# Choosing 128 of 144 keys by the 16 left out, and moving small steps around the pairs of an attention block

## The chip, the cores and the metric

The kernel runs on one core of a Trainium2 chip. The metric is the device time of one execution in microseconds, as the median of several. TensorE, VectorE, ScalarE, GpSimd and SyncE each work through their own list of instructions in order and wait for one another by semaphores.

## The reference, cut to what matters

Two blocks follow one another on 512 tokens of width 1024: a gated-linear-attention mixer and a state-space mixer, then a transformer block with 16 meta tokens ahead (528 tokens), whose mixer has 8 dense causal heads and 8 heads that see only 128 chosen keys. The part that the change touches:

```python
topk = min(TOPK_MAX, seq // 4)                       # 128
logits = einsum('bqhd,bkd->bqhk', q_idx, k_idx) * idx_scale
score = einsum('bqh,bqhk->bqk', w_idx, relu(logits))
score = where(causal, score, -inf)
_, sel = lax.top_k(score, topk)
valid = sel <= qpos
s = einsum('bqhd,bqkhd->bhqk', q, k[sel]) * scale    # also for the dense heads, without sel
p = softmax(where(valid, s, -inf))
o = einsum('bhqk,bqkhd->bqhd', p, v[sel])
h = h + concat(o_mla, o_dsa) @ w_o                   # h: the residual, rms-normed x of the first block
h = h + swiglu(rmsnorm(h)); out = rmsnorm(h)
```

## The kernel before, in words

Activations lie with features on the 128 partitions and tokens along the free axis. A product is three matmuls of split parts (lines 728 to 730), and each output tile goes to one of two banks of PS by turns: `open_tile` waits until the tile before the last has been read out (`slot_free`). Weights come through a ring of slots; ScalarE makes their high part (L1515), GpSimd (L2890) or VectorE (L2162) the low part.

The attention block, in the order of TensorE: query tiles of the index (qi), kk and ckv, cq and qs, beside which the 20 index scores stand (L1207); then ks, vs (three tiles), uqr (two), uqn (four), ukn (four), ukvv (three), and the 32 pairs of heads (`PAIRS`): four tiles of 128 queries, which see 144, 272, 400 and 528 keys, and for each 4 dense (mla) and 4 sparse (dsa) pairs; the first tile has its sparse pairs first.

Index scores: TensorE makes `index_scores(n)`, when relu n - 1 is done; ScalarE's relu (L1934) of score n waits for VectorE's sums of score n - 2 (`summed_up`, `acc_used`); VectorE sums into `acc`, one row of keys per query. Score units 0 to 3 are the queries 0 to 127, 4 to 7 the second tile, 8 to 11 the third, 12 to 19 the fourth. After unit 15's round VectorE splits a weight.

Choice (`select`): a round is MAX8, which finds the 8 largest of a row, and MATCH_REPLACE, which sets them to `TAKEN`. 16 rounds for each of the four tiles find 128 keys. After the last, two instructions (L2725, L2726) turn the row into a mask that also is causal. 8 rounds stand behind units 12 to 19, 32 behind the rotations (`rotate`, L2667 to L2677) of QS, KR, KS and QR, and 24 in the pairs 3 to 26, one each.

ScalarE after the index: ks (L1912), vs (L1972), QR (`evac`, L1538, with the split of the next weight ahead of the wait), a copy of the rotary keys KR to four heads' rows of Km in two steps (`rotary_keys`, L1976), the second after the first tile of Qm (L1987, L1988), then Km (L1995).

A pair p: TensorE makes the scores of p (L1315 dense, L1317 sparse), the transposes of p - 2 (L1353), the product with values of p - 3 (L1365). VectorE copies the output of p - 4 to OA (L2765), adds the mask and finds the maximum (L2784), makes a round of choice (p = 3 to 26), two reciprocals of the sums (L2771), each after its exponential, and for p = 23 to 30 scales one tile of the residual XT (L2796). ScalarE makes two exponentials (L2002) and copies the transposed weights of p - 2 (L2022, L2024). GpSimd scales the two heads by the reciprocals (L2916). The transposes of a 528-key tile also wait for the copy to OA of the pair two before them.

Then attn_out: 8 tiles, each added to XT by VectorE (L2822), which frees the bank, then the sums of squares and the split for the next stage. The first two tiles are computed side by side.

Of the kernel before, what the change touches and what calls it, by code (L numbers as in the profile page):

```python
# [2 lines left out]

# [1 line left out]

# [7 lines left out]
ALU = mybir.AluOpType  # L13
ACT = mybir.ActivationFunctionType
# [6 lines left out]
KD = D // P  # L21
# [6 lines left out]
NPAIR = T // P  # L28
# [29 lines left out]
TOPK = 128  # L58
# [3 lines left out]
LOW = -1e30  # L62
TAKEN = -3e38
# [13 lines left out]
PV_GLA, PV_BG, PV_HG, PV_S5, PV_BGLU, PV_DS, PV_FIN, PV_ATT, PV_GQ, PV_GKV, PV_FFN, PV_FIN2, PV_N = \  # L77
# [81 lines left out]
def build(nc, a, out):  # L159
# [105 lines left out]
    tiles = plan.tiles  # L265
# [23 lines left out]
    PLAIN, plain_at = {}, 0  # L289
# [7 lines left out]
    with ExitStack() as ctx:  # L297
# [25 lines left out]
        pv = keep("pv", [P, PV_N])  # L323
# [5 lines left out]
        rs1 = keep("rs1", [P, T])  # L329
# [4 lines left out]
        st = keep("st", [P, 3, 8])  # L334
        xt_off = top[0] + 31 & -32
        XT = keep("XT", [P, KD, T])
# [115 lines left out]
        VS, o = place("VS", [P, 5, DH * DHD], o)  # L452
# [3 lines left out]
        top8, o = place("top8", [P, 8], o)  # L456
        mx, o = place("mx", [P, 6, 4], o)
# [34 lines left out]
        PS = ctx.enter_context(nc.psum_tensor("PS", [P, 4, 512], F32))  # L492
# [6 lines left out]
        tile_done = sem("tile_done")  # L499
# [61 lines left out]
        def keys(i):  # L561

            return NM + (i + 1) * P
# [16 lines left out]
        FIRST_QS = len(ROTATIONS)  # L580
# [23 lines left out]


        OUT_SPLIT, FIRST_CHOICE = len(PAIRS) - 8, 3
        XT_PAIR = len(PAIRS) - KD - 1

        z_dram = nc.dram_tensor("z_gates", (DI, T), F32, kind="Internal").ap()
        g_dram = nc.dram_tensor("glu_parts", (DI, T), F32, kind="Internal").ap()  # L610
# [88 lines left out]
        def norm_applied(eng, name):  # L699

            if name == "ck":
                eng.wait_ge(xlo_ready, sum(SPLITS["ckv"]))
            elif name in SPLITS:
                eng.wait_ge(xlo_ready, sum(SPLITS[name]))
            else:
                eng.wait_ge(normed, PLAIN[name] + NORMS[name][2])
# [755 lines left out]
        def act_program(act):  # L1462
# [45 lines left out]
            def split_weights(upto):  # L1508


                while done[0] <= min(upto, len(plan.loads) - 1):
                    n = done[0]
                    done[0] += 1
                    act.wait_ge(landed[n % NSLOT], plan.value[n])
                    act.activation(ring_hi[:, n % NSLOT, 0:plan.size[n]], ring[:, n % NSLOT, 0:plan.size[n]], ACT.Copy)\  # L1515
                        .then_inc(whi_ready, 1)
# [448 lines left out]
            for i, tile in enumerate(tiles["ks"]):  # L1965
                wide(tile, KS[:, i, :])

            for i, tile in enumerate(tiles["vs"]):
                split_weights(tile.loads[-1] + 1)
                act.wait_ge(tile_done, tile.t + 1)  # L1970
                for b in range(2 if i < 2 else 1):
                    m = act.activation(VS[:, 2 * i + b, :], PS[:, 2 * tile.slot + b, :], ACT.Copy, scale=st[:, 2, 2 * i + b:2 * i + b + 1])  # L1972
                m.then_inc(slot_free[tile.slot], 1)
            def rotary_keys(j):

                ins = act.activation(Km[MNOPE:MQK, 2 * j:2 * j + 2, :],  # L1976
                                     KR[MNOPE:MQK, :].unsqueeze(1).broadcast_to([MROPE, 2, T2]), ACT.Copy)
                if j == 1:
                    ins.then_inc(kr_copied, 1)

            for i, tile in enumerate(tiles["uqr"]):
                evac(tile, QR[:, i, :], scale=-MQK ** -0.5)
            act.wait_ge(roped, KEYS_TURNED)
            rotary_keys(0)
            for i, tile in enumerate(tiles["uqn"]):
                act.wait_ge(tile_done, tile.t + 1)
                act.activation(Qm[0:MNOPE, 2 * i, :], PS[0:64, 2 * tile.slot, 0:T], ACT.Copy, scale=-MQK ** -0.5)  # L1987
                act.activation(Qm[0:MNOPE, 2 * i + 1, :], PS[64:P, 2 * tile.slot, 0:T], ACT.Copy, scale=-MQK ** -0.5)\  # L1988
                    .then_inc(slot_free[tile.slot], 1)
                if i == 0:  # L1990
                    rotary_keys(1)
            for i, tile in enumerate(tiles["ukn"]):
                act.wait_ge(tile_done, tile.t + 1)
                for h in range(2):
# [104 lines left out]
        def dve_program(dve):  # L2099
            chain = [0]  # L2100

            def link(ins):

                chain[0] += 1
                ins.then_inc(dve_chain, 1)
                dve.wait_ge(dve_chain, chain[0])
# [584 lines left out]
            def acc_of(i):  # L2691
                return acc[:, ACC_AT[i]:ACC_AT[i + 1]]

            def causal(i):
                return rt[:, C_CB + T2 - keys(i):C_CB + T2]

            def summed_up(n):
                i, hp, c0, w = INDEX[n]
                dve.wait_ge(relu_ready, n + 1)
                here = acc_of(i)[:, c0:c0 + w]  # L2700
                for h in range(2):
                    of, weight = RL[:, n % 2, h, 0:w], WI[:, i, 2 * hp + h:2 * hp + h + 1]
                    if hp == h == 0:
                        link(ts(here, of, weight, None, ALU.mult))
                    else:
                        ins = stt(out=here, in0=of, scalar=weight, in1=here, op0=ALU.mult, op1=ALU.add)
                        if h == 0:
                            link(ins)
                ins.then_inc(acc_used, 1)
                dve.wait_ge(acc_used, n + 1)  # L2710
                if hp == 3 and c0 + w == keys(i):
                    link(tt(acc_of(i), acc_of(i), causal(i), ALU.subtract))

# [1 line left out]

            def select(rounds):
                for _ in range(rounds):
                    i, last = chosen[0] // (TOPK // 8), chosen[0] % (TOPK // 8) == TOPK // 8 - 1  # L2720
                    chosen[0] += 1
                    link(dve.max(top8[:], acc_of(i)))
                    link(dve.match_replace(out=acc_of(i), in_to_replace=top8[:], in_values=acc_of(i), imm_value=TAKEN))
                    if last:
                        link(ts(acc_of(i), acc_of(i), TAKEN, 1.0, ALU.is_equal, ALU.subtract))  # L2725
                        link(stt(out=acc_of(i), in0=acc_of(i), scalar=LOW, in1=causal(i), op0=ALU.mult, op1=ALU.add))  # L2726

# [21 lines left out]
            low("ckv", 0, ssq[:, 0:T2], CKh[:, 0:T2], CKl[:, 0:T2])  # L2749
            for n in range(12, len(INDEX)):  # L2750
                summed_up(n)
                select(1)
                if n == 15:
                    low_weights(tiles["ks"][0].loads[0])
            for n, rounds in zip(range(FIRST_QS, len(ROTATIONS)), (5, 5, 4, 4, 4, 4, 3, 2, 1, 0, 0)):
                rotate(n)
                select(rounds)

# [7 lines left out]
                    .then_inc(oa_ready, 1)  # L2766

            def inverse_sums(p):
                for n in (2 * p, 2 * p + 1):
                    dve.wait_ge(exp_ready, n + 1)  # L2770
                    dve.reciprocal(mx[:, n % 6, 2:3], mx[:, n % 6, 1:2]).then_inc(rsum_ready, 1)  # L2771

            dve.wait_ge(pb_zero, 1)
            for p, (kind, i, hp) in enumerate(PAIRS):
                if p >= 4:
                    output(p - 4)
                nk = keys(i)
                bias = causal(i) if kind == "mla" else acc_of(i)
                dve.wait_ge(score_ps, p + 1)
                if p >= 3:  # L2780
                    dve.wait_ge(pT_ps, p - 2)
                for h in range(2):
                    n = 2 * p + h
                    dve.tensor_tensor_reduce(split(PB[:, n % 6, 0:nk], i), scores(p, h), split(bias, i), 1.0, -TAKEN, ALU.add, ALU.min,  # L2784
                                             mx[:, n % 6, 0:1]).then_inc(reduced, 1)
                if p == 1:
                    tile = tiles["ukvv"][2]
                    dve.wait_ge(tile_done, tile.t + 1)
                    dve.tensor_copy(Vm[:, 4, :], PS[:, 2 * tile.slot, :]).then_inc(slot_free[tile.slot], 1)
                if 0 <= p - FIRST_CHOICE < 3 * TOPK // 16:  # L2790
                    select(1)
                inverse_sums(p)
                if 0 <= p - XT_PAIR < KD:

                    k = p - XT_PAIR
                    stt(out=XT[:, k, :], in0=XT[:, k, :], scalar=pv[:, PV_FIN + k:PV_FIN + k + 1], in1=rs1[:], op0=ALU.mult, op1=ALU.mult)\  # L2796
                        .then_inc(normed, 1)
            assert chosen[0] == NPAIR * (TOPK // 8)
            output(len(PAIRS) - 4)

            for n in (2 * len(PAIRS) - 2, 2 * len(PAIRS) - 1):
# [14 lines left out]

            for i in range(4, KD):
                low("oa", i, OA[:, i, :], OAh[:, i, :], OAl[:, i, :])
            norm_applied(dve, "fin")
            for i, tile in enumerate(tiles["attn_out"]):  # L2820
                dve.wait_ge(tile_done, tile.t + 1)
                tt(XT[:, i, :], XT[:, i, :], PS[:, 2 * tile.slot, :], ALU.add).then_inc(slot_free[tile.slot], 1)  # L2822
                sum_squares("ffn", i - 1)
                if i > 0:
                    ffn_low(i - 1)
# [237 lines left out]
```

## Time and profile before

| what | us |
|---|---|
| median of 3 runs (lowest to highest) | 1667.53 (1667.22 to 1667.67) |
| span of the profiled execution | 1664.5 |
| TensorE busy | 1625.8 (98%) |
| VectorE busy | 1003.7 (60%) |
| ScalarE busy | 713.9 (43%) |
| GpSimd busy | 474.9 (29%) |

The profiled execution has no run time of its own beside its span; the runs of the kernel lie some 3 us above it. Mean granted TensorE clock 0.996. The attention block's part that the change touches lies from 1040 to 1240 us. Shares of busy time are means over stages with different limits; what ends a wait is read in the waits and timelines. In the rows, the first number is the start in us from the span's start, the second the time in us; `x2` is a merged group of two; what stands in brackets is the idle time of that engine ahead of the row and what ended it. PE is TensorE, DVE VectorE, ACT ScalarE, POOL GpSimd.

### The profile page before, as it was taken

The numbers are of one execution on the slowest core, as the hardware profiler recorded it, in microseconds if no ns is written. First come the engines' busy times: TensorE is split into PE (matmuls) and PEld (weight loads), VectorE is DVE, ScalarE is ACT, GpSimd is POOL, SyncE is SP. The second block draws the span as 40 slices with busy tenths as digits, with TensorE's granted clock in tenths as the row PEclk, the third lists the DMA queues.
The fourth block names the chain that finished last, engine by engine and source line by source line (L and its number), as shares of the span: only waits on it lengthen the run. The fifth ranks groups of instructions, "written<-read, shape, count | busy, mean of one in ns | idle before, by whom it ended". The sixth has DMA issues, their size and how long they took to land.

```text
span 1664.5 us, 24805 instructions
## 1 busy us (share of the span) xinstructions
PE 1625.8 (98%) x10072; PEld 1296.2 (78%) x10072; DVE 1003.7 (60%) x1569; ACT 713.9 (43%) x1112; POOL 474.9 (29%) x169
## 2 busy tenths in 40 slices
PE   9999999999999998999999999999999999999998
PEld 7778688888778786778887886786778888888887
DVE  4356635786999999984672755998963212222123
ACT  4482433334555567655433333327763322222122
POOL 2221124342000000000434431234773344344332
PEclk9999999999999999999999999999999999999999
DMA  5232013235655454556643321221003333322322
GB/s 177 77 101 76 27 52 99 79 101 162 141 145 142 123 150 114 119 137 212 225 134 115 101 74 52 76 57 52 1 1 102 92 86 101 101 80 80 99 87 86
DMA packets 268311, 167.98 MB, mean 101 GB/s; under 512 B 90811, under 2 KB 248854, under 8 KB 268070
## 3 DMA queue, kind: packets, MB, share of 16 engines
q1 hardware_dynamic: 256592, 146.45, 31.6%
q10 hardware_dynamic: 11158, 18.08, 3.2%
q0 software_dynamic: 448, 1.88, 0.3%
q8 instruction: 80, 1.31, 0.3%
q14 instruction: 33, 0.27, 0.1%
HBM read 144.87 MB, written 16.78 MB: 97 GB/s over the span
## 4 chain that ended last, share of the span: by engine, by line
PE 82%; DVE 9%; SPq 3%; ACT 3%; issue 1%; DMA 1%; ACTq 0%; DVEq 0%
PE PS L728 23%; PE PS L729 23%; PE PS L730 23%; SPq L2945 2%; SPq L2955 1%; PE PS L1365 1%; PE PA L957 1%; DVE ring_lo L2162 1%; PE PS L1353 1%; PE PA L981 1%; PE PA L1315 1%; PE PA L1194 1%; PE PA L985 1%; PE PA L1080 1%; DMA KM<-GS 1%
## 5 line engine op out<-in xcount | busy, mean ns | idle before, releaser
L2890 POOL TENSOR_TENSOR ring_lo<-ring,ring_hi 128x2048 fp32r<-128x2048 f32 (+2 forms) x90 | 393.8, 4376 | 1103.7 <-ACT ring_hi L1515 1101.2
L1515 ACT ACTIVATE ring_hi<-ring 128x2048 fp32r<-128x2048 f32 (+2 forms) x121 | 221.0, 1827 | 205.9 <-PE PS L730 167.7
L729 PE MATMUL PS<-U3l,ring_hi 128*128 128x512 f32 x352 | 139.9, 397 | 0.0
L728 PE MATMUL PS<-U3h,ring_hi 128*128 128x512 f32 x352 | 139.4, 396 | 0.0
L730 PE MATMUL PS<-U3h,ring_lo 128*128 128x512 f32 x352 | 138.9, 395 | 0.0
L2833 DVE TENSOR_TENSOR SF<-PS,rs 128x512 f32<-128x512 f32 x22 | 15.2, 691 | 162.7 <-PE PS L730 162.7
L728 PE MATMUL PS<-HT5h,ring_hi 128*128 128x512 f32 x256 | 105.5, 412 | 0.0
L730 PE MATMUL PS<-HT5h,ring_lo 128*128 128x512 f32 x256 | 101.4, 396 | 0.0
L729 PE MATMUL PS<-HT5l,ring_hi 128*128 128x512 f32 x256 | 101.2, 395 | 0.0
L2063 ACT ACTIVATE SF<-SF 128x512 f32<-128x512 f32 x22 | 13.9, 631 | 171.1 <-DVE SF L2833 171.1
L2162 DVE TENSOR_TENSOR ring_lo<-ring,ring_hi 128x2048 fp32r<-128x2048 f32 x31 | 70.5, 2286 | 18.6 <-ACT ring_hi L1515 18.5
L2916 POOL TENSOR_SCALAR PB<-PB,mx 128x144 f32<-128x144 f32 (+3 forms) x62 | 70.0, 1142 | 34.4 <-DVE mx L2771 34.4
L728 PEld LDWEIGHTS PS<-U3h,ring_hi 128*128 128x128 f32 x352 | 66.3, 188 | 16.4
L730 PEld LDWEIGHTS PS<-U3h,ring_lo 128*128 128x128 f32 x352 | 66.1, 188 | 16.1
L729 PEld LDWEIGHTS PS<-U3l,ring_hi 128*128 128x128 f32 x352 | 66.2, 188 | 15.2
L728 PE MATMUL PS<-HFh,ring_hi 128*128 128x512 f32 (+1 forms) x198 | 74.1, 374 | 0.0
L729 PE MATMUL PS<-HFl,ring_hi 128*128 128x512 f32 (+1 forms) x198 | 73.3, 370 | 0.0
L730 PE MATMUL PS<-HFh,ring_lo 128*128 128x512 f32 (+1 forms) x198 | 73.1, 369 | 0.0
L728 PE MATMUL PS<-HTh,ring_hi 128*128 128x512 f32 x176 | 70.4, 400 | 1.5 <-ACT QG L1538 1.5
L729 PE MATMUL PS<-HTl,ring_hi 128*128 128x512 f32 x176 | 69.8, 396 | 0.0
L730 PE MATMUL PS<-HTh,ring_lo 128*128 128x512 f32 x176 | 69.7, 396 | 0.0
L728 PE MATMUL PS<-U2hf,ring_hi 128*128 128x512 f32 (+2 forms) x176 | 63.2, 359 | 0.2 <-ACT RL L1934 0.2
(509 smaller groups left out, 4091.6 us busy)
## 6 DMA issues: line engine op xcount, KB each, us to landing
ring<-in_gla_w_in SPq DMA_DIRECT2D x20, 1024.0 KB, 5.2
ring<-in_s_w_in SPq DMA_DIRECT2D x16, 1024.0 KB, 6.0
ring<-in_s_w_glu SPq DMA_DIRECT2D x16, 1024.0 KB, 5.8
ring<-in_w_gate SPq DMA_DIRECT2D x22, 512.0 KB, 4.0
ring<-in_w_up SPq DMA_DIRECT2D x22, 512.0 KB, 5.2
ring<-in_w_down SPq DMA_DIRECT2D x16, 704.0 KB, 4.5
ring<-in_w_in SPq DMA_DIRECT2D x9, 1024.0 KB, 5.2
ring<-in_gla_w_out SPq DMA_DIRECT2D x8, 1024.0 KB, 5.6
```

Source lines behind the costliest of these rows:

```text
L728: pe.matmul(dst, w[0], x[0], start=start, stop=False)
L729: pe.matmul(dst, w[0], x[1], start=False, stop=False)
L730: return pe.matmul(dst, w[1], x[0], start=False, stop=stop)
L957: pe.matmul(PA[:, (n - 1) % 2, :], KE[r, tt, h * P:(h + 1) * P], V[r, tt, h * GDV:(h + 1) * GDV], start=True, stop=True).then_inc(kv_ps, 1)
L981: pe.matmul(bank[rows, :], V[:, tt, es], ATT[:, h, tt * P:(tt + 1) * P], start=True, stop=False)
L985: m = pe.matmul(bank[rows, r], S[:, (c - 1) % 3, es], QG[:, h, c * GCH:(c + 1) * GCH], start=False, stop=c == 2 * tt + 1)
L1080: pe.matmul(to[h], UB[:, b % 2, g, :], KM[b % 2][:, g, h * 64:(h + 1) * 64], start=True, stop=False)
L1515: act.activation(ring_hi[:, n % NSLOT, 0:plan.size[n]], ring[:, n % NSLOT, 0:plan.size[n]], ACT.Copy)\
L2162: tt(ring_lo[:, n % NSLOT, at], ring[:, n % NSLOT, at], ring_hi[:, n % NSLOT, at].bitcast(F32), ALU.subtract).then_inc(wlo_dve, 1)
L2890: pool.tensor_tensor(ring_lo[:, n % NSLOT, at], ring[:, n % NSLOT, at], ring_hi[:, n % NSLOT, at].bitcast(F32), ALU.subtract).then_inc(wlo ...
L2916: pool.tensor_scalar(PB[:, n % 6, 0:nk], PB[:, n % 6, 0:nk], mx[:, n % 6, 2:3], None, ALU.mult).then_inc(p_ready, 1)
L2945: sp.dma_start(UB[s * SGRP:(s + 1) * SGRP, b % 2], src[s]).then_inc(ub_in[b % 2], 16)
```

## The change

- Queries 0 to 127 see 144 keys, of which 128 are to be chosen. The causal mask minus the score is built instead of the score minus the mask, so that two rounds mark the 16 that are left out, in reversed order of keys (`[:, ::-1]`) for ties; the closing two instructions are of the same kinds. The tile takes 2 rounds instead of 16, all tiles 50 instead of 64.
- Ahead of the pairs stand 26 rounds instead of 40: behind index scores 12 to 17, and 3, 3, 3, 3, 2, 2, 2, 1, 1 behind the rotations. The pairs 3 to 26 keep one round each.
- While rounds are left in the pairs (p = 0 to 25), one reciprocal serves both heads of a pair and waits for both exponentials.
- The scaling of XT leaves the pairs 23 to 30 and stands ahead of each output tile's sum in attn_out.
- ScalarE's two copies of the rotary keys stand directly behind the last value tile, ahead of uqr's evacuations.

```diff
-        XT_PAIR = len(PAIRS) - KD - 1
+        ROUNDS_TO = list(itertools.accumulate([(keys(0) - TOPK) // 8] + [TOPK // 8] * (NPAIR - 1)))
...
+            act.wait_ge(roped, KEYS_TURNED)
+            rotary_keys(0)
+            rotary_keys(1)
             for i, tile in enumerate(tiles["uqr"]):
                 evac(tile, QR[:, i, :], scale=-MQK ** -0.5)
-            act.wait_ge(roped, KEYS_TURNED)
-            rotary_keys(0)
...
-                if i == 0:
-                    rotary_keys(1)
...
-                    link(tt(acc_of(i), acc_of(i), causal(i), ALU.subtract))
+                    if i == 0:
+
+                        link(tt(acc_of(i), causal(i), acc_of(i), ALU.subtract))
+                    else:
+                        link(tt(acc_of(i), acc_of(i), causal(i), ALU.subtract))
...
-                    i, last = chosen[0] // (TOPK // 8), chosen[0] % (TOPK // 8) == TOPK // 8 - 1
+                    i = next(i for i in range(NPAIR) if chosen[0] < ROUNDS_TO[i])
                     chosen[0] += 1
+                    last = chosen[0] == ROUNDS_TO[i]
+
+                    taken_from = acc_of(i)[:, ::-1] if i == 0 else acc_of(i)
                     link(dve.max(top8[:], acc_of(i)))
-                    link(dve.match_replace(out=acc_of(i), in_to_replace=top8[:], in_values=acc_of(i), imm_value=TAKEN))
-                    if last:
+                    link(dve.match_replace(out=taken_from, in_to_replace=top8[:], in_values=taken_from, imm_value=TAKEN))
+                    if last and i == 0:
+                        link(ts(acc_of(i), acc_of(i), TAKEN, -LOW, ALU.is_equal, ALU.mult))
+                        link(tt(acc_of(i), acc_of(i), causal(i), ALU.add))
+                    elif last:
...
                 summed_up(n)
-                select(1)
+                select(1 if n < 18 else 0)
...
-            for n, rounds in zip(range(FIRST_QS, len(ROTATIONS)), (5, 5, 4, 4, 4, 4, 3, 2, 1, 0, 0)):
+            for n, rounds in zip(range(FIRST_QS, len(ROTATIONS)), (3, 3, 3, 3, 2, 2, 2, 1, 1, 0, 0)):
...
             def inverse_sums(p):
-                for n in (2 * p, 2 * p + 1):
-                    dve.wait_ge(exp_ready, n + 1)
-                    dve.reciprocal(mx[:, n % 6, 2:3], mx[:, n % 6, 1:2]).then_inc(rsum_ready, 1)
+                if chosen[0] < ROUNDS_TO[-1]:
+                    dve.wait_ge(exp_ready, 2 * p + 2)
+                    both_heads = slice(2 * p % 6, 2 * p % 6 + 2)
+                    dve.reciprocal(mx[:, both_heads, 2:3], mx[:, both_heads, 1:2]).then_inc(rsum_ready, 2)
+                else:
+                    for n in (2 * p, 2 * p + 1):
+                        dve.wait_ge(exp_ready, n + 1)
+                        dve.reciprocal(mx[:, n % 6, 2:3], mx[:, n % 6, 1:2]).then_inc(rsum_ready, 1)
...
-                if 0 <= p - XT_PAIR < KD:
-
-                    k = p - XT_PAIR
-                    stt(out=XT[:, k, :], in0=XT[:, k, :], scalar=pv[:, PV_FIN + k:PV_FIN + k + 1], in1=rs1[:], op0=ALU.mult, op1=ALU.mult)\
-                        .then_inc(normed, 1)
...
-            norm_applied(dve, "fin")
             for i, tile in enumerate(tiles["attn_out"]):
+                stt(out=XT[:, i, :], in0=XT[:, i, :], scalar=pv[:, PV_FIN + i:PV_FIN + i + 1], in1=rs1[:], op0=ALU.mult, op1=ALU.mult)\
+                    .then_inc(normed, 1)
+                dve.wait_ge(normed, PLAIN["fin"] + i + 1)
                 dve.wait_ge(tile_done, tile.t + 1)
                 tt(XT[:, i, :], XT[:, i, :], PS[:, 2 * tile.slot, :], ALU.add).then_inc(slot_free[tile.slot], 1)
```

## Rows read from the trace of the kernel before

**Rows 1.** Waits of TensorE, 1040 to 1240 us: line, releaser, us, times, longest.

```profile
PE PS L1353 <- ACT PT L2022: 2.8, 7, 1.0
PE PS L1353 <- ACT PT L2024: 1.4, 2, 1.0
PE PA L1207 <- ACT RL L1934: 1.0, 3, 0.5
PE PS L728 <- ACT Km L1995: 0.9, 3, 0.3
```

**Rows 2.** Timeline of ScalarE and VectorE in pairs 13 and 19.

```profile
1165.86 0.52 ACT L2002 ACTIVATE PB<-PB,mx 128x272 f32<-128x272 f32 x1 [0.78 <-DVE mx L2784]
...
1182.81 0.57 DVE L2784 CUSTOM_DVE_ANT_0 PB<-PA,rt 128x400 f32<-128x400 f32 x1 [0.27 <-PE PA L1315]
```

**Rows 3.** Timeline of VectorE: a round on 144 keys, the closing, a round on 272.

```profile
1047.74 0.31 DVE L2722 MAX8 top<-acc 128x8 f32<-128x144 f32 x1
...
1048.49 1.02 DVE L2706 SCALAR_TENSOR_TENSOR acc<-RL,WI,acc 128x264 f32<-128x264 f32 x2
...
1082.51 0.23 DVE L2725 TENSOR_SCALAR acc<-acc 128x144 f32<-128x144 f32 x1
...
1083.12 0.45 DVE L2722 MAX8 top<-acc 128x8 f32<-128x272 f32 x1
...
1088.10 0.45 DVE L2722 MAX8 top<-acc 128x8 f32<-128x272 f32 x1
...
1089.11 0.45 DVE L2722 MAX8 top<-acc 128x8 f32<-128x272 f32 x1
```

**Rows 4.** Timeline at the last index scores: relu 18, score 19, first key tile.

```profile
1057.09 0.61 ACT L1934 ACTIVATE RL<-PA 128x528 f32<-128x528 f32 x1 [2.66 <-DVE acc L2706]
...
1057.76 0.72 PE L1207 MATMUL PA<-KI__145,QI 64*128 64x264 f32 x4 [0.16 <-ACT RL L1934]
...
1059.57 0.40 PE L728 MATMUL PS<-U2hf,ring_hi 128*128 128x264 f32 x1 [0.20 <-ACT RL L1934]
```

**Rows 5.** Timelines of ScalarE, and of TensorE at uqn's first tile, 1120 to 1131 us.

```profile
1120.85 0.58 ACT L1538 ACTIVATE QR<-PS 128x512 f32<-128x512 f32 x1
...
1122.51 1.08 ACT L1976 ACTIVATE Km<-KR 32x1056 f32<-32x1056 f32 x1
...
1129.21 0.59 ACT L1987 ACTIVATE Qm<-PS 64x512 f32<-64x512 f32 x1 [0.20 <-PE PS L730]
...
1130.44 4.98 ACT L1995 ACTIVATE Km<-PS 64x528 f32<-64x528 f32 x8
...
1121.69 0.39 PE L728 MATMUL PS<-CQh,ring_hi 128*128 128x512 f32 x1
```

**Rows 6.** Timeline of VectorE: two reciprocals together, and one alone.

```profile
1149.76 0.22 DVE L2771 RECIPROCAL mx<-mx 128x1 f32<-128x1 f32 x2
...
1213.80 0.16 DVE L2771 RECIPROCAL mx<-mx 128x1 f32<-128x1 f32 x1 [0.56 <-ACT PB L2002]
```

**Rows 7.** Timeline of VectorE and TensorE in pairs 26 to 28.

```profile
1210.63 0.73 DVE L2796 SCALAR_TENSOR_TENSOR XT<-XT,pv,rs 128x512 f32<-128x512 f32 x1
...
1211.28 0.28 DVE L2765 COPY OA<-PS 128x128 f32<-128x128 f32 x1
...
1211.67 1.28 PE L1353 MATMUL PS<-con,PB 128*128 128x128 f32 x10 [0.81 <-issue]
...
1217.74 1.15 DVE L2796 SCALAR_TENSOR_TENSOR XT<-XT,pv,rs 128x512 f32<-128x512 f32 x1
```

**Rows 8.** Timeline: VectorE beside GpSimd at 1061, GpSimd in the pairs, both at attn_out.

```profile
1061.40 5.43 DVE L2706 SCALAR_TENSOR_TENSOR acc<-RL,WI,acc 128x264 f32<-128x264 f32 x2
...
1210.75 13.30 POOL L2916 TENSOR_SCALAR PB<-PB,mx 128x528 f32<-128x528 f32 x8 [1.42 <-DVE mx L2771]
...
1239.64 9.34 POOL L2890 TENSOR_TENSOR ring_lo<-ring,ring_hi 128x2048 fp32r<-128x2048 f32 x2 [4.42 <-ACT ring_hi L1515]
...
1247.30 1.32 DVE L2822 TENSOR_TENSOR XT<-XT,PS 128x512 f32<-128x512 f32 x2 [7.50 <-PE PS L730]
```

More of the change, by code:

```diff
@@ L2 @@
 from contextlib import ExitStack
+import itertools
 import numpy as np
@@ L1966, in act_program, with rotary_keys @@
                 wide(tile, KS[:, i, :])
+            def rotary_keys(j):
+                ins = act.activation(Km[MNOPE:MQK, 2 * j:2 * j + 2, :],
+                                     KR[MNOPE:MQK, :].unsqueeze(1).broadcast_to([MROPE, 2, T2]), ACT.Copy)
+                if j == 1:
+                    ins.then_inc(kr_copied, 1)
             for i, tile in enumerate(tiles["vs"]):
@@ L1973, in act_program @@
                 m.then_inc(slot_free[tile.slot], 1)
[L1974 to L1979, printed above, removed]
+            act.wait_ge(roped, KEYS_TURNED)
+            rotary_keys(0)
+            rotary_keys(1)
             for i, tile in enumerate(tiles["uqr"]):
                 evac(tile, QR[:, i, :], scale=-MQK ** -0.5)
-            act.wait_ge(roped, KEYS_TURNED)
-            rotary_keys(0)
             for i, tile in enumerate(tiles["uqn"]):
@@ L2789, in dve_program @@
                     dve.tensor_copy(Vm[:, 4, :], PS[:, 2 * tile.slot, :]).then_inc(slot_free[tile.slot], 1)
-                if 0 <= p - FIRST_CHOICE < 3 * TOPK // 16:
+                if p >= FIRST_CHOICE and chosen[0] < ROUNDS_TO[-1]:
                     select(1)
                 inverse_sums(p)
-                if 0 <= p - XT_PAIR < KD:
-                    k = p - XT_PAIR
-                    stt(out=XT[:, k, :], in0=XT[:, k, :], scalar=pv[:, PV_FIN + k:PV_FIN + k + 1], in1=rs1[:], op0=ALU.mult, op1=ALU.mult)\
-                        .then_inc(normed, 1)
-            assert chosen[0] == NPAIR * (TOPK // 8)
+            assert chosen[0] == ROUNDS_TO[-1]
             output(len(PAIRS) - 4)
```

## Prediction

> **What bounds the kernel now.** I read the page first: TensorE is busy 98% of the 1664.5 us span, so a change counts only where TensorE stands still, or by what it makes it stand still. Then the waits of TensorE over the stretch that the change touches, 1040 to 1240 us: transposes (L1353) wait 2.8 us in 7 places and 1.4 us in 2 for ScalarE's copy of the transposed weights; index scores (L1207) wait 1.0 us for the relu; the key tiles wait 0.9 us for ScalarE's copies into Km [rows 1]. TensorE's standstill here is some 7 us in all, these four rows 6.1 of it. Then the timelines of VectorE, ScalarE and TensorE in that stretch, to see which engine stands behind each wait. They show four parts. Index scores (to 1060 us): VectorE hardly pauses and is late. Keys, values, up-projections (1060 to 1130): VectorE is full, yet TensorE never waits. Up-projection of the keys (1130 to 1136): ScalarE is late. Pairs (1136 to 1236): VectorE is late in pairs 4 to 14, TensorE itself is the bound in pairs 15 to 25 (VectorE's reduction waits for its scores, as at 1182.81), VectorE is late again for a few of the last nine [rows 2].
>
> **The 14 rounds of choice that go.** A round on 144 keys takes 0.75 us (1047.74 to 1048.49), one on 272 takes 1.01 us [rows 3]. Before, 40 rounds ran ahead of the pairs (16 on 144 keys, 16 on 272, 8 on 400); after, 26 (2, 16, 8). VectorE loses 14 x 0.75 = 10.5 us there. But 24 rounds run in the pairs before and after, at the same pairs and widths, and TensorE does not wait for VectorE between 1060 and 1130. The rotations behind the removed rounds hand QS, KS and KR to the first scores, at 1135.87, long after. What bounds the last rotations is their own four copies to Qm, which start only when TensorE has turned QR. So I take 0 us for the 10.5 us: VectorE will idle instead. If rotation were on the path, it could bring at most the standstill of the key tiles around 1130, 0.9 us; that is the bound on that side.
>
> **The order of rounds inside the index scores: a cost.** Scores 12 to 19 are summed with a round behind each. After, score 12 has a round of queries 0 to 127, score 13 another plus the two closing instructions, 0.61 us from 1082.51 to 1083.12 [rows 3], scores 14 to 17 each a 272-key round, 0.26 us longer than today's, 18 and 19 none. Before score 16's sums VectorE is later by 0.61 + 2 x 0.26 = 1.13 us, before score 17's by 1.39 us (14 to 16 have three of them). Relu 18 waits for the sums of score 16 (2.66 us of idleness, ended by acc), score 19 waits for relu 18, and the first key tile at 1059.57 for relu 19, with no slack at either [rows 4]. The relus of scores 16 and 17 have slack (ScalarE had other work ahead). So TensorE goes on 1.4 us later. Bounds: 0 if I mistook a slack, 1.9 if the two reversed replacements take double. Value +1.4.
>
> **ScalarE's copies of the rotary keys: a cost.** Two copies of 1.08 us (1.10 from start to start) stood behind QR's evacuations and between those of Qm. Now both come directly behind the last value tile, ahead of the evacuation of uqr's first tile, and of the weight split that stands before it. That evacuation starts at 1120.85 and frees the bank for uqn's first tile, which TensorE opens at 1121.69; the slack is 0.3 us. With 2 x 1.10 ahead, TensorE waits 2.2 - 0.3 = 1.9 us. ScalarE does the same work in sum, but today it was waiting for TensorE as late as 1129.21 (0.20 us), behind which its copies to Km run without a pause (from 1130.44) and set TensorE's waits: so all 1.9 us reach the first scores [rows 5]. Queued behind the two copies on ScalarE are the weight split (for ukn, slack of 3 us), QR, Qm, Km. Their own wait is met by then: KR is turned ahead of all of KS. Bounds 1.7 and 2.1. Value +1.9.
>
> **Shared reciprocals: a gain where VectorE is late.** Two reciprocals keep VectorE 0.22 us, one 0.16 [rows 6]: 0.06 a pair. In pairs 4 to 14 each pair's reduction stands behind it (ScalarE idles 0.78 us for it each time, [rows 2]); one of the nine is lost at the change to 272 keys, where the scores take over. 9 x 0.06 = 0.5 us. In pairs 15 to 25 it brings nothing. The added wait for both exponentials costs nothing in the pairs with a round, since they end during the round; in pairs 0 to 2 GpSimd starts the first head 0.4 us later, and TensorE waits there for the copy of Vm. Bounds 0.3 and 1.5 (24 pairs). Value -0.5.
>
> **The residual's scaling leaves pairs 23 to 30: a gain.** Each of 8 takes 0.73 us (1.15 once). They stand ahead of the copy to OA, for which TensorE's transposes of 528-key queries wait. At 1211.67 the transposes stood 0.81 us, the copy being at 1211.28 behind the scaling of 1210.63: 0.65 us comes free, of which nothing is late next but VectorE itself [rows 7]. The stretched scaling at 1217.74 held the next but one by 0.33 us, part of the 1.4 us of [rows 1]. Sum -1.0. Elsewhere the scores are later than the copy. Bounds -0.6 and -1.3. Put beside the output tiles, each scaling is done while VectorE waits: it waits 7.5 us ahead of the first sum [rows 8], and ahead of the later ones for as long as TensorE takes to a tile less its own two or three instructions; the cover for the first is discussed below. Were that cover gone, each would cost its 0.73 us. Cost 0.
>
> **Sum.** +1.4 + 1.9 - 0.5 - 1.0 = +1.8 us. The rest of the kernel is TensorE's, so it carries over whole. The profiled execution has a span of 1664.5 and the runs lie at 1667.2 to 1667.7, so 3 us lie around it: 1666.3 in a profile, 1667.5 + 1.8 = 1669.3 us as a median.
>
> **A lock between VectorE and GpSimd.** What rows show: VectorE's sums of score 19, with both inputs in SBUF, took 5.43 us for two instead of 1.02, until GpSimd's weight split (started 1061.95) was done. Two such splits run without a gap from 1239.64 to 1248.98, and the scaling of XT's first tile now falls into the first of them. If VectorE gets its turn between the two (1244.3), it is done at 1245.0, ahead of the tile's sum at 1247.30. If GpSimd's second split goes first, the scaling ends at 1249.7, the sum at 1250.4 instead of 1248.0, and TensorE, which opened the third tile 0.2 us behind that sum, stands 2.4 us more [rows 8]. I hold the first for likelier, as VectorE's instruction has been waiting by then. [...]
>
> **Rivals.** (1) VectorE's time is worth something: the index stage isn't late, waits around 1130 vanish, all 24 pairs gain, and the rotary copies find slack. The 1.0 of index waits, 0.9 around 1130, 1.5 and 1.3 in the pairs: up to -4.7 us, 1662.8. For it: VectorE is over 90% busy from 1045 to 1136. Against: TensorE's waits for it in the middle are zero. (2) Slower: the lock goes to GpSimd at 1244.3, 1669.3 + 2.4 = 1671.7. It decides from 1247.3 on: up to there everything is covered. For it: the splits are back to back. (3) The reordering inside the index scores or on ScalarE costs nothing, since an engine takes it up that I haven't seen: 1667.9 or 1667.4. (4) The shared reciprocal takes as long as two: 1669.8, not to be told from the forecast.
>
> **How the numbers follow.** What a measurement of this kernel can tell from no change is about 0.2%, 3.3 us. The forecast with (3) and (4), all within that, holds 0.80; (1) 0.08; (2) 0.12. The bounds of the terms give -1.1 (0 + 1.7 - 1.5 - 1.3) and +3.1 (1.9 + 2.1 - 0.3 - 0.6), 1666.4 to 1670.6; it takes in (2) above, and a little below for (1): 1665.8 to 1671.8.
>
> **What would show it.** In the changed profile: VectorE idle for some 10 us between 1070 and 1136; waits of L1207 and of the first key tile up by 1.4 us; a new wait of uqn's first tile of some 1.9 us, ended by ScalarE's QR; the first scores at about 1139 instead of 1135.9; pairs from first scores to first output tile shorter by 1.5 us; no pause of 0.8 us at pair 27. Wrong if the first scores come before 1136.5, if the pairs shorten by over 3 us, or if the third output tile waits over 1 us.

## The result and the profile after

The changed kernel takes 1671.5 us, the kernel before 1667.6 beside it (medians of 22 runs of each, 3.9 us apart). The ratio is 1.0026, with a 95% interval of 1.0018 to 1.0033, which makes 4.3 us more. Run again later, beside another set of runs of the kernel before, it was 1.0012 (1.0001 to 1.0022). It is slower by 0.1 to 0.3%, where 1669.3 us and a difference of 1.8 us were forecast.

The page of the changed kernel, its span and first part:

```profile
span 1673.0 us, 24747 instructions
PE 1629.9 (97%) x10072; PEld 1300.1 (78%) x10072; DVE 994.2 (59%) x1501; ACT 713.6 (43%) x1112; POOL 474.5 (28%) x169
```

VectorE's busy time fell by 9.5 us (1003.7 before), and nothing came of it. That this is near the 10.5 us of the 14 rounds is chance: the kernel with the rounds alone has 989.6 us, 14.1 less. In the busy time stand single instructions of VectorE that took several times their usual time beside a split of GpSimd, and they differ between the kernels. Before, two sums of score 19 took 5.43 us instead of 1.02, so that the 14 instructions of that shape (128x264) come to 11.3 us of busy time (6.9 in the changed kernel), and one step of the rotations of QS took 4.98 instead of 0.69. In the changed kernel the subtraction of the mask on 528 keys (L2719, at 1069.34 us) took 5.13 us instead of 0.71, and the scaling of XT's first tile 5.12 instead of 0.73. The span is 8.5 us longer than the 1664.5 of before, but most of that lies ahead of anything that the change touches: the attention block's first query product starts at 967.19 us, 7.45 us later than in the profile before. Positions from the span's start can't be compared, so all further reading is by stretches between four starts of TensorE, each found in a timeline. The changed kernel's:

```profile
967.19 0.39 PE L732 MATMUL PS<-U2hf,ring_hi 128*128 128x512 f32 x1
...
1126.49 0.40 PE L732 MATMUL PS<-CQh,ring_hi 128*128 128x512 f32 x1
...
1145.41 0.52 PE L1321 MATMUL PA<-KS,QS 64*128 64x144 f32 x4
...
1244.85 0.51 PE L732 MATMUL PS<-OAh,ring_hi 128*128 128x512 f32 x1
```

These are the first query product, the first uqr product, the first pair's scores and the first attn_out product. They make stretch A (index, keys, values), B (up-projections, where ScalarE's order changed) and C (the pairs). The rest, D, runs from attn_out to the last product on its normed result. In us, from one profiled execution of each kernel:

| kernel | A | B | C | D |
|---|---|---|---|---|
| before | 159.15 | 16.98 | 100.52 | 292.9 |
| changed | 159.30 | 18.92 | 99.44 | 293.0 |
| changed, again | 159.30 | 18.96 | 99.50 | 292.9 |
| rotary copies alone | 157.67 | 18.95 | 100.56 | 292.9 |
| rounds alone | 159.30 | 16.99 | 100.49 | 292.9 |
| reciprocals and scaling alone | 157.65 | 17.04 | 99.61 | 292.9 |
| scaling alone | 157.64 | 16.98 | 99.55 | 292.9 |
| reciprocals alone | 157.61 | 16.98 | 100.52 | 292.9 |
| changed, rotary copies put back | 159.28 | 16.99 | 99.45 | 292.9 |
| no rounds beside the index | 157.15 | 16.98 | 99.45 | 293.0 |
| the same again | 157.16 | 16.98 | 99.45 | 292.9 |
| thirty rounds ahead, again | 157.16 | 16.98 | 99.11 | 293.0 |
| no choice in the pairs | 157.66 | 16.97 | 96.97 | 293.0 |

One entry misleads: A of the kernel before. TensorE's granted clock fell there in that one execution (to 0.66 from 1025 to 1030 us, below). The five kernels whose index part is that of before and which had the full clock there give 157.61 to 157.67, so 157.65 stands for before. Then the change costs 1.65 us in A and 1.94 in B, and brings 1.08 in C: +2.5 us, a ratio of 1.0015, by the first profile, +2.6 by the second.

The waits of TensorE in the changed kernel, 1036 to 1250 us, answer to [rows 1]:

```profile
PE PS L1357 <- ACT PT L2025: 2.5, 6, 1.0
PE PA L1211 <- ACT RL L1938: 2.1, 3, 1.3
PE PS L732 <- ACT QR L1542: 1.7, 1, 1.7
PE PS L1357 <- ACT PT L2027: 1.0, 1, 1.0
...
PE PS L732 <- ACT Km L1998: 0.9, 3, 0.3
PE PS L732 <- ACT RL L1938: 0.5, 1, 0.5
...
PE PS L732 <- POOL ring_lo L2905: 0.2, 1, 0.2
```

The waits for the relu RL grew by 1.1 us at the index scores (1.0 before) and by 0.3 at the first key tile ([rows 4] has 0.20): together the forecast 1.4. The wait for QR, 1.7 us, is new. The wait for GpSimd's ring_lo, 0.2 us, is new too, and nothing in the prediction has it. The transposes (L1357, before L1353) are listed with 0.3 and 0.4 us less. These places on the timelines, of ScalarE, TensorE and GpSimd:

```profile
1064.19 0.61 ACT L1938 ACTIVATE RL<-PA 128x528 f32<-128x528 f32 x1 [3.53 <-DVE acc L2709]
...
1064.85 0.72 PE L1211 MATMUL PA<-KI__145,QI 64*128 64x264 f32 x4 [1.29 <-ACT RL L1938]
...
1095.57 4.87 POOL L2905 TENSOR_TENSOR ring_lo<-ring,ring_hi 128x2048 fp32r<-128x2048 f32 x1 [8.46 <-ACT ring_hi L1519]
...
1100.49 0.51 PE L732 MATMUL PS<-ring_hi,U2hf 128*128 128x512 f32 x1 [0.19 <-POOL ring_lo L2905]
...
1127.40 2.06 ACT L1974 ACTIVATE Km<-KR 32x1056 f32<-32x1056 f32 x2
...
1131.17 0.47 PE L732 MATMUL PS<-CQh,ring_hi 128*128 128x512 f32 x1 [1.71 <-ACT QR L1542]
```

Relu 18 waits 3.53 us for VectorE instead of 2.66, and TensorE 1.29 for it instead of 0.16 [rows 4]. Both rotary copies run in one piece from 1127.40, and uqn's first tile waits 1.71 us for the evacuation behind them.

### The profile page after: what moved, and what is told of

The parts are those of the page before. It is cut to its first block, busy times and chain, and to the rows that moved or that the text cites. A ratio compares the mean times of both kernels' runs of the same rounds, so it can differ in the third digit from the quotient of the medians.

```text
span 1673.0 us, 24747 instructions
## 1 busy us (share of the span) xinstructions
PE 1629.9 (97%) x10072; PEld 1300.1 (78%) x10072; DVE 994.2 (59%) x1501; ACT 713.6 (43%) x1112; POOL 474.5 (28%) x169
## 4 chain that ended last, share of the span: by engine, by line
PE 80%; DVE 11%; ACT 3%; SPq 3%; issue 1%; DMA 1%; POOL 0%; DVEq 0%; ACTq 0%; POOLq 0%
PE PS L732 23%; PE PS L733 22%; PE PS L734 22%; SPq L2960 2%; DVE ring_lo L2165 1%; PE PS L1369 1%; PE PA L961 1%; SPq L2970 1%; PE PS L1357 1%; PE PA L985 1%; PE PA L1319 1%; PE PA L989 1%; PE PA L1198 1%; PE PA L1084 1%; PE PA L1086 1%
```

## The experiments

**The rotary copies alone.** The kernel before, with both copies directly behind the value tiles:

```diff
+            act.wait_ge(roped, KEYS_TURNED)
+            rotary_keys(0)
+            rotary_keys(1)
             for i, tile in enumerate(tiles["uqr"]):
                 evac(tile, QR[:, i, :], scale=-MQK ** -0.5)
```

> The kernel before with one part of the change: ScalarE's two copies of the rotary keys directly behind the last value tile. My theory (they delay the first evacuation of uqr by 2 x 1.10 us, slack 0.3): the first tile of uqn waits 1.7 to 1.9 us for ScalarE's QR, the first scores come 1.9 us later, the pairs keep their 100.5 us, and the time rises by 1.9 us, ratio 1.0011. Rival (ScalarE has room and takes it up): no such wait, ratio 1.0000.

B went from 16.98 to 18.95, everything else stayed. Ratio 1.001 (0.9999 to 1.0021). Its waits of TensorE hold the one new row, and the waits of Km that follow are as long as before:

```profile
PE PS L728 <- ACT QR L1538: 1.7, 1, 1.7
...
PE PS L728 <- ACT Km L1994: 0.9, 3, 0.3
```

So ScalarE doesn't make the time good behind the copies: 1.97 us for a move of two instructions. The whole time alone could not show it, as the interval just reaches 1.

**The rounds alone.** The changed kernel with rotary copies, reciprocals and scaling as before; what is left is the choice by the 16 left out and 26 rounds ahead of the pairs.

> The kernel before with the choice alone changed: 2 rounds for the first queries, six rounds beside the index scores (four of them on 272 keys), 20 behind the rotations. My theory: index scores and first key tile wait 1.4 us longer, VectorE idles 10 us or more before the pairs, nothing is gained by that: ratio 1.0008. Rival (VectorE's 10.5 us are worth something): ratio below 0.999. Second rival, for the 2.5 us that the change costs beyond my sum: the lighter VectorE shifts something else that TensorE waits for, ratio 1.002 or more.

A is 159.30, 1.65 more than 157.65; B and C are those of before. Ratio 1.0 (0.9986 to 1.0013), too wide to tell 1.65 us. VectorE lost its 14 rounds here (busy 989.6 us instead of 1003.7) and C didn't shorten.

**Reciprocals and scaling alone, then each by itself.** The kernel before, with one reciprocal for both heads (while p < 26) and the scaling of XT ahead of each output tile's sum; then two kernels with one of them each.

```diff
+                if p < 26:
+                    dve.wait_ge(exp_ready, 2 * p + 2)
+                    both_heads = slice(2 * p % 6, 2 * p % 6 + 2)
+                    dve.reciprocal(mx[:, both_heads, 2:3], mx[:, both_heads, 1:2]).then_inc(rsum_ready, 2)
```

> The kernel before with the shared reciprocals (pairs 0 to 25) and the residual's scaling beside the output tiles alone. My theory: the stretch from first scores to first output tile shortens from 100.5 by 1.1 to 1.5 us, the third output tile waits no more than before: ratio 0.9992. Rival (a lock between VectorE and GpSimd at the output tiles): the third output tile waits over 2 us, ratio 1.0005 or more.

C is 99.61, ratio 0.9998 (0.9987 to 1.0009). The gain of 0.91 us was less than the two terms' 1.5, and less than the 1.1 expected at least, hence the two kernels apart:

> The kernel before with the shared reciprocals alone. After the profile of the changed kernel (copy to OA 0.86 us behind the start of MATCH_REPLACE in pair 13, before 0.87) my theory is that one reciprocal of two columns keeps VectorE as long as two of one: the stretch from first scores to first output tile is 100.4 us, 0.1 less than before. My sum on record had 0.5 us less; then it would be 100.0.

> The kernel before with the residual's scaling beside the output tiles alone. Theory: it is all of the pairs' gain: first scores to first output tile 99.6 us (100.5 before), the third output tile waits 0.2 us as before. Rival (the gain comes only with the shared reciprocals): 100.0 or more.

The reciprocals alone give C = 100.52, as before: nothing. The scaling alone gives 99.55, -0.97 us. So the scaling is the whole of it. Why the shared reciprocal brings nothing is seen on VectorE in a pair with a round on 528 keys, of the kernel with the reciprocals alone, and of the kernel before:

```profile
1166.63 0.69 DVE L2723 MATCH_REPLACE8 acc<-top,acc 128x528 f32<-128x528 f32 x1
1167.41 0.17 DVE L2772 RECIPROCAL mx<-mx 128x2 f32<-128x2 f32 x1
1167.50 0.27 DVE L2765 COPY OA<-PS 128x128 f32<-128x128 f32 x1
```

```profile
1164.33 0.69 DVE L2723 MATCH_REPLACE8 acc<-top,acc 128x528 f32<-128x528 f32 x1
1165.06 0.22 DVE L2771 RECIPROCAL mx<-mx 128x1 f32<-128x1 f32 x2
1165.20 0.27 DVE L2765 COPY OA<-PS 128x128 f32<-128x128 f32 x1
```

The one reciprocal starts 0.78 us after the start of MATCH_REPLACE8, the first of the two 0.73; the copy to OA starts after 0.87 us in both. The durations, 0.17 and 0.22, differ by what the starts give back. The spacing of the next instruction is what a pair pays, and that did not change. It is the same within 0.01 us in 22 of the 23 pairs that have a round and a shared reciprocal; in the last the copy waited for something else. The list of TensorE's waits has 0.3 us less for the transposes in this kernel too (2.5 us in 6 places instead of 2.8 in 7); mostly this is a wait of 0.18 us, at 1149.81 in the kernel before, that isn't listed here. C has none of it, so it is the stretch and not the list of waits that says what was gained.

**The changed kernel again.**

> The changed kernel itself, to see how its time and its granted clock vary beside the kernel before on one chip. If the trace's waits are all there is (sum of the parts +2.4 us), the ratio is 1.0014, and what it shows beyond that goes with a lower granted clock. If a part is missing from my sum, the ratio is 1.0026 at the same clock.

1671.7 us against 1668.8 for the kernel before (35 runs): 1.0012 (1.0001 to 1.0022). The four stretches are those of the first profile within 0.06 us each, while the first query product starts 3.83 us earlier (963.36).

**The changed kernel with the rotary copies where they were.**

> The changed kernel with ScalarE's copies of the rotary keys where they were. If the parts add up: first uqr product to first scores 17.0 us instead of 18.9, index stretch (first s5-normed query product to first uqr product) 159.3 us and pairs 99.5 us as in the changed kernel. If VectorE's lead is what makes the early copies useful, some of the 1.9 us stays.

B is 16.99, A and C are the changed kernel's: the parts don't act on each other. Its one time, 1672.2 us, is no lower than the changed kernel's, with a mean granted clock of 0.994 and a first query product at 966.58: a single run can't show 2 us in this kernel, its stretches can.

**No rounds beside the index.** The last kernel, with the rounds behind the index scores moved to the rotations, where VectorE idles:

```diff
             for n in range(12, len(INDEX)):
                 summed_up(n)
-                select(1 if n < 18 else 0)
...
-            for n, rounds in zip(range(FIRST_QS, len(ROTATIONS)), (3, 3, 3, 3, 2, 2, 2, 1, 1, 0, 0)):
+            for n, rounds in zip(range(FIRST_QS, len(ROTATIONS)), (4, 4, 4, 3, 3, 3, 2, 2, 1, 0, 0)):
```

> The changed kernel with the rotary copies back and none of the 26 rounds beside the index scores, all behind the rotations, into VectorE's idle time. My theory: the index stretch falls from 159.3 us to 157.4 (before, without a slow clock: 157.7), rotations stay off the path, pairs 99.5 us, in all 1.2 us less than the kernel before: ratio 0.9993. Rival (VectorE gets late at the rotations): the first scores wait for VectorE, over 17.0 us from uqr to them.

> The version with the rotary copies back and no round beside the index scores once more, on this chip, beside the next: 1.9 us less than the kernel before by the stretches of its first profile, ratio 0.9989. If its first ratio (0.9988) was chance, it lies at 1.000.

A is 157.15 and 157.16, 2.1 us below the changed kernel and 0.5 below the kernel before. TensorE's wait for the relus in the index scores:

```profile
PE PA L1211 <- ACT RL L1938: 0.7, 2, 0.4
```

Times: 1666.0 us, ratio 0.9988 (0.9977 to 0.9998), and 1666.4, ratio 0.9993 (0.9982 to 1.0003). By the stretches this kernel is 1.6 us faster than before (0.50 in A, 1.07 in C), a ratio of 0.9990, which both intervals hold; the 1.2 and 1.9 us of the two expectations lie on either side of it. The 1.07 is the scaling's, so only the 0.50 comes from the rounds. No kernel moved the rounds with the list of all 64 kept, so it is argued, not shown, that the shorter list is what makes room for them. VectorE still idles ahead of the rotations, so there is room for more.

**Thirty rounds ahead of the pairs.** The same kernel with 30 rounds behind the rotations, `(3, 4, 4, 4, 4, 3, 3, 1, 4, 0, 0)`, and the 20 others in the pairs from 7 on (`FIRST_CHOICE = 7`).

> As the one before, with 30 rounds ahead of the pairs, so that pairs 3 to 6 have none. My theory (VectorE bounds the first pairs, and its idle time ahead of them is the only thing that the 14 rounds less can buy): first scores to first output tile 98.3 us instead of 99.5, uqr to first scores still 17.0, ratio 0.9986. Rival (VectorE has no room ahead, or ScalarE's chain bounds the first pairs): the first is unchanged at 99.5, or the scores come later by what VectorE is late.

> The version with 30 rounds ahead of the pairs once more: 0.3 us less than the one before by its stretches, ratio 0.9987. If the moved rounds cost something outside the stretches that I measured, it is the slower of the two by 0.1% as in the first comparison.

C is 99.09 and 99.11, 0.35 us less than 99.45 for four rounds taken out of the first pairs. The expectation had 98.3, a gain of 1.2 us, most of which didn't come. In these pairs VectorE's reduction then waits for the scores and ScalarE's exponential for the reduction by turns:

```profile
1150.72 0.41 ACT L2006 ACTIVATE PB<-PB,mx 128x144 f32<-128x144 f32 x1 [0.33 <-DVE mx L2802]
...
1152.41 0.31 DVE L2802 CUSTOM_DVE_ANT_0 PB<-PA,rt 128x144 f32<-128x144 f32 x1 [0.33 <-PE PA L1319]
```

Ratios 0.9993 (0.9983 to 1.0002) and 0.9994 (0.9982 to 1.0005). The first profile of this kernel has A at 158.65, with a fall of the clock in it; the second 157.16. It can't be told in time from the kernel with no rounds beside the index. Both lie some 0.1% below the kernel before, at the edge of what these runs can tell.

**No choice in the pairs.** The kernel before without the 24 rounds in the pairs; it leaves part of the choice out, and only its times are of use:

```diff
-                if 0 <= p - FIRST_CHOICE < 3 * TOPK // 16:
-                    select(1)
```

> The kernel before without the 24 rounds of choice in the pairs (part of the choice is left out). It measures what VectorE's rounds cost in the pairs at most. Theory (late in pairs 4 to 14 only, by 0.2 to 0.9 us each): first scores to first output tile 93 to 96 us. Rival (ScalarE's copies and exponentials are the bound just behind VectorE): over 98 us.

C is 96.97: 24 rounds on 400 and 528 keys, each 1.3 to 1.6 us of VectorE and over 30 us together, are worth 3.55 us. That lies between the theory (93 to 96) and the rival (over 98), and neither has it right. The transposes' waits fell, but some stayed:

```profile
PE PS L1353 <- ACT PT L2024: 1.1, 1, 1.1
...
PE PS L1353 <- ACT PT L2022: 0.8, 2, 0.6
```

The 3.55 us are the price of the choice in the pairs as a whole, and so about the most that a change of the choice can bring there. VectorE's other work in the pairs is still in this kernel.

## Why the prediction was right or wrong, step by step

**TensorE bounds the kernel, VectorE's 10.5 us are worth 0: right.** In the changed kernel VectorE is busy 56.3 us of the 77.5 from the first key tile to the first scores, where it was busy 72.4 of 76.0. Its group of rotations in that stretch (busy, mean ns, idle time before them and what ended it):

```profile
L2670 DVE TENSOR_TENSOR ro<-PA,rt 128x512 f32<-128x512 f32 (+2 forms) x11 | 7.7, 699 | 17.3 <-PE PA L1198 17.2
```

It waits 17.2 us for TensorE's rotation products, more than the 10 forecast. Of the 14 rounds that this stretch lost, four were on 272 keys (10 x 0.75 + 4 x 1.01 = 11.5), and the stretch itself grew by 1.5 us. Of the rest, 4.3 us are one step of the rotations of QS, which in the kernel before (the first row) once took 4.98 us, at 1075.36 while a split of GpSimd ran, and in the changed kernel (the second) never does:

```profile
L2672 DVE TENSOR_TENSOR QS<-QS,ro 128x512 f32<-128x512 f32 x4 | 7.1, 1764 | 0.1
```

```profile
L2675 DVE TENSOR_TENSOR QS<-QS,ro 128x512 f32<-128x512 f32 x4 | 2.8, 692 | 0.1
```

Rival (1), that this time is worth something, fell: B and C of the kernel with the rounds alone are those of before. And TensorE's waits for Km stayed at 0.9 us, so the rotations don't bound them. One reading was short: the standstill of "some 7 us" is 7.9 in the list of waits, since 1.2 us of the transposes without a named releaser, the pause at pair 27 among them, are not in [rows 1].

**The order of rounds in the index scores, +1.4: right in mechanism, 0.25 short.** A grew by 1.65 us. 1.4 is what the waits of the relus give: 1.13 more for relu 18 (0.16 to 1.29), which is the 0.61 + 2 x 0.26 of the prediction, and 0.26 more at the first key tile (0.20 to 0.46). 0.19 comes from a place that the forecast had called free, TensorE's wait at 1100.49 for GpSimd's low part of a weight. That split took 4.87 us, and 4.60 in the kernel before. VectorE, then GpSimd of the changed kernel, and GpSimd of the kernel before:

```profile
1095.27 0.69 DVE L2675 TENSOR_TENSOR QS<-QS,ro 128x512 f32<-128x512 f32 x1
```

```profile
1088.21 4.60 POOL L2890 TENSOR_TENSOR ring_lo<-ring,ring_hi 128x2048 fp32r<-128x2048 f32 x1 [8.43 <-ACT ring_hi L1515]
```

With the shorter list VectorE's step of the rotation (1095.27 to 1095.96) has begun when GpSimd's split is issued at 1095.57, and the split takes 0.27 us longer; in the kernel before VectorE was in MAX8 of a round at 1088.21 [rows 3: the round of 1088.10]. I had read from TensorE's zero waits for VectorE that nothing between 1060 and 1130 could cost; [rows 8] had shown the two engines in each other's way (5.43 us instead of 1.02), but with VectorE as the one that waits. The same split takes 4.85 to 4.87 us in every kernel with the shorter list and 4.59 to 4.61 in every one with the old list. That the overlap is the reason is read from these rows, no kernel tried it alone. The remaining 0.06 has no row. The kernel without rounds beside the index keeps the wait for ring_lo (0.18 us), yet its A is 2.14 us shorter than the changed kernel's: its relu waits fell from 2.59 to 0.70 us, where the kernel before has 1.19. So the relus' part of the 1.65 goes away with the rounds, and 0.49 of the old waits with it; the other 0.2 has no row.

**Rotary copies, +1.9: right.** 1.94 to 1.98 in B, in the changed kernel, its repeat and the kernel with the copies alone, and a wait of 1.71 us at the tile named, ended by QR. That tile starts 4.68 us after the first uqr product instead of 2.80. Rival (3), that an engine takes up one of the two moves, fell with this kernel and with the one that has the rounds alone.

**Shared reciprocals, -0.5: wrong.** This is rival (4), which held: 0.00 us. The step that failed took the difference of two durations (0.22 and 0.16, [rows 6]) as time on the path. It had compared a reciprocal of one column with two of one column, and durations instead of the distance between the starts of the instructions around them. (It also counts nine pairs, where 4 to 14 are eleven; at nothing a pair this doesn't matter.)

**The residual's scaling, -1.0 in the pairs: right.** -0.97 by itself. TensorE's pause at pair 27 shrank from 0.81 us [rows 7] to 0.47:

```profile
1220.43 0.74 PE L1357 MATMUL PS<-con,PB 128*128 128x128 f32 x5 [0.47 <-issue]
```

**Beside the output tiles, 0, and VectorE's turn between the splits: right.** GpSimd's two splits and VectorE's scaling of the first tile meet as foreseen. That VectorE's instruction took 5.12 us instead of 0.73 beside them is in the rows; that a lock does it was my reading and no run shows it:

```profile
1248.10 9.67 POOL L2905 TENSOR_TENSOR ring_lo<-ring,ring_hi 128x2048 fp32r<-128x2048 f32 x2 [4.42 <-ACT ring_hi L1519]
...
1248.18 5.12 DVE L2833 SCALAR_TENSOR_TENSOR XT<-XT,pv,rs 128x512 f32<-128x512 f32 x1
...
1255.77 0.69 DVE L2837 TENSOR_TENSOR XT<-XT,PS 128x512 f32<-128x512 f32 x1 [2.47 <-PE PS L734]
...
1256.60 0.47 PE L732 MATMUL PS<-OAh,ring_hi 128*128 128x512 f32 x1 [0.24 <-DVE XT L2837]
```

The scaling is done at 1253.30, 0.55 us after the end of the first split (1252.75) and well ahead of that of the second (1257.77); the pair took 9.67 us instead of 9.34. VectorE then still waits 2.47 us for the first tile, and the third output tile waits 0.24 us, as before. One thing the prediction hadn't seen: the second tile's scaling meets the second split (until 1257.77) and takes 1.94 us instead of 0.73, so that the second sum starts at 1258.35, and no longer right behind the first. It costs nothing, since TensorE is at the third tile until then:

```profile
1256.37 1.94 DVE L2833 SCALAR_TENSOR_TENSOR XT<-XT,pv,rs 128x512 f32<-128x512 f32 x1
```

Rival (2), the slower one at 1671.7 us, fell, though the measured time is near its number: none of its mechanism is in the profile. D is 292.9 to 293.0 in all kernels.

**The sum: two of its terms failed.** Measured in stretches: +1.65 + 1.95 + 0.00 - 1.05 = +2.55 us, against +1.8. The shared reciprocals were put at -0.5 and brought 0.00; the order of rounds in the index scores was put at +1.4 and cost 1.65. So the change costs 2.55 us, 1.4 times the forecast, and the rest of the measured 4.3 us isn't in the stretches at all. The 2.55 us alone would have lain below the 0.2% (3.3 us) that I took as the bound of what can be told.

**From 2.5 to the measured 4.3 us.** The runs of each kernel spread by about 10 us, and the spread follows the granted clock: over all runs, with a level of its own for each kernel, 0.001 more of mean granted clock goes with 1.39 us less, and what is left scatters by 1.6 us. The kernel before had a mean of 0.9954 (the 79 runs beside the experiments; for the 22 of the first comparison only the times are on record), the changed one 0.9947 (22 runs) in the first comparison and 0.9950 in the second. Against these 79 runs, at equal clock, the two sets of the changed kernel give +2.4 (standard error 0.4) and +2.2 us (0.5), which is the sum of the stretches. So of the 1.9 us by which the first comparison exceeds these, about 1.0 (0.0007 x 1390) goes with a lower clock. Of the other 0.9, 0.7 is that the 22 runs of the kernel before in that comparison have a mean of 1667.7 us, the 79 others one of 1668.4; with what clock they ran isn't known, so this part stays open. Whether the changed kernel brings the lower clock about or the runs fell so can't be settled: its second set of runs is nearer to before.

Where the clock falls differs from execution to execution, in code that the change doesn't touch. Stretches of 25 us of the changed kernel, then the same two of the kernel before (columns: stretch, length, busy us of TensorE, its weight loads, VectorE, ScalarE, GpSimd, then the granted clock, DMA share, GB/s):

```profile
425.00:450.00 25.00, 21.34 (x212) 16.87 (x211) 23.01 (x26) 9.71 (x21) 0.00 (x0) 0.93 0.54 125
1025.00:1050.00 25.00, 25.00 (x155) 15.47 (x154) 15.10 (x25) 12.49 (x21) 4.55 (x1) 1.00 0.26 84
```

```profile
425.00:450.00 25.00, 22.70 (x226) 18.00 (x225) 24.12 (x27) 12.22 (x25) 0.00 (x0) 1.00 0.63 149
1025.00:1050.00 25.00, 24.64 (x104) 14.45 (x102) 18.30 (x33) 11.92 (x18) 4.57 (x1) 0.93 0.14 42
```

A mean of 0.93 is one piece of 5 us at 0.66 and four at 1.00, in both kernels. In the changed kernel the piece lies from 440 to 445 us, and in the 5 us before it TensorE was busy for only 1.74, with the DMA engines at 0.80 of their time:

```profile
435.00:440.00 5.00, 1.74 (x11) 1.05 (x10) 4.79 (x7) 2.40 (x2) 0.00 (x0) 1.00 0.80 195
440.00:445.00 5.00, 5.00 (x17) 3.92 (x16) 4.97 (x6) 2.55 (x3) 0.00 (x0) 0.66 0.90 198
```

In the kernel before TensorE was busy 3.12 of 5 us in the longest pause there, and the clock stayed. At 1025 us of the kernel before, the clock fell (to 0.66 in the first 5 us) with TensorE busy in all of the 25 us ahead, and that goes with 1.5 us more in its stretch A (159.15 against 157.65); the first profile of the kernel with thirty rounds ahead shows the same. What starts these falls was not tried.

**What I would have had to put into the range.** That 1671.5 lies inside the stated range of 1665.8 to 1671.8 is luck: the bounds of the terms ended at 1670.6, and the range went further for rival (2), which didn't happen. "3 us lie around it" mixed two things: a run takes 1.8 us more than its own span (2.1 in the kernel with reciprocals and scaling alone), and the other 1.2 us was that the profiled execution of before was a quick one. And the chance of a difference above 3.3 us lacked the scatter of means from the clock, some 1 us here.

## What to carry to other kernels

Before moving a step forward on an engine, look at the evacuation that it is put ahead of: two copies of 1.1 us cost 1.95 us here, though the engine does the same work, while 10.5 us less work on an engine ahead of a stage that TensorE bounds brought nothing by itself; moving other work (the rounds beside the index scores) into the idle time brought 0.5. For the gain of a merged small instruction, measure from start to start of its neighbours, not its duration. And compare kernels of such a length by stretches between landmarks, with the granted clock beside each: at the full clock they repeat within 0.1 us, while whole runs scatter by 10.

## What the runs showed of the hardware that was not expected

- Beside two splits of GpSimd that stood back to back, VectorE's scaling got its turn between them: it started at 1248.18, 0.08 us behind the first, and took 5.12 us instead of 0.73. The first split ended at 1252.75, the scaling at 1253.30, the second split at 1257.77.
- GpSimd's scalings in the pairs didn't hold VectorE up in this way. In the kernel before, the scaling of XT at 1221.40 starts and ends inside one of them and takes its usual 0.73 us, and the one at 1217.74 (1.15 us) is done at 1218.89, before GpSimd's instruction of 1217.64 to 1219.24 is. So VectorE stood until the end of GpSimd's instruction at the splits here, and not at the scalings:

```profile
1220.86 1.60 POOL L2916 TENSOR_SCALAR PB<-PB,mx 128x528 f32<-128x528 f32 x1
```

```profile
1221.40 0.73 DVE L2796 SCALAR_TENSOR_TENSOR XT<-XT,pv,rs 128x512 f32<-128x512 f32 x1
```

- It reads as if VectorE holds GpSimd up too: GpSimd's split took 4.87 instead of 4.60 us when it was issued 0.30 us behind the start of VectorE's step of the rotation, and TensorE stood 0.19 for it. The scaling of GpSimd at 1210.75 of the kernel before, issued 0.12 us behind the start of one of VectorE's, took 2.09 us instead of 1.60.
- Replacing in reversed order of keys cost VectorE nothing. In the changed kernel, where it is reversed for the first tile, MATCH_REPLACE8 on 144 keys takes 0.29 us, as in the kernel before (0.29 at 1048.16):

```profile
1055.92 0.29 DVE L2733 MATCH_REPLACE8 acc<-top,acc 128x144 f32<-128x144 f32 x1
```
